# Attention on one core: the order of two PE steps of a unit, the values product and the spreading of 1/l

## What is computed

```
s = q @ k.T * SCALE + bias(head)           # causal, or dilated windows
p = exp(s - max(s)); l = sum(p)            # per query
out = (p @ v) / l
```

## Time and profile before

| what | value |
|---|---|
| median of 3 runs | 2630.19 us (2628.05 to 2633.6) |
| the profiled execution: its time, its span | 2626.38 us, 2624.3 us |
| mean granted TensorE clock | 0.992 of full speed |
| busy: PE, DVE, ACT, POOL | 97%, 43%, 21%, 42% |

### The profile page before, as it was taken

How to read it: one execution, slowest core, us unless ns; L and a number is a source line. 1 busy time by engine, 2 the same in 40 slices (tenths; PEclk the granted TensorE clock), 3 DMA queues, 4 the chain that set the end, 5 groups by cost and what they waited for, 6 DMA issues and landing times.

```text
span 2624.3 us, 42745 instructions
## 1 busy us (share of the span) xinstructions
PE 2556.8 (97%) x16331; PEld 2344.0 (89%) x16331; DVE 1133.9 (43%) x2258; ACT 550.1 (21%) x1266; POOL 1101.6 (42%) x702
## 2 busy tenths in 40 slices
PE   7999989999999999999999999899999999999999
PEld 5777756666899999999999987899999999999999
DVE  6636536667344333333333360553733333333333
ACT  5201136666322000000000051322300000000001
POOL 4234115566665444333344262435654443333440
PEclk9999999999999999999999999999999999999999
DMA  5223148767312111111111111111121111111111
GB/s 158 70 80 91 60 129 247 217 203 211 96 34 73 49 43 45 44 44 48 48 48 48 33 49 32 49 33 49 33 65 48 44 43 45 43 48 48 48 32 65
DMA packets 218459, 189.83 MB, mean 72 GB/s; under 512 B 29443, under 2 KB 171523, under 8 KB 217956
## 3 DMA queue, kind: packets, MB, share of 16 engines
q1 hardware_dynamic: 200996, 161.89, 21.2%
q10 hardware_dynamic: 17344, 26.35, 2.8%
HBM read 171.19 MB, written 17.01 MB: 72 GB/s over the span
## 4 chain that ended last, share of the span: by engine, by line
PE 69%; DVE 2%; POOL 2%; ACT 1%; issue 1%; ACTq 0%; POOLq 0%; PEldq 0%; DVEq 0%
PE ps L536 63%; PE ps L566 1%; PE ps L568 1%; PE ps L567 1%; ACT ps L2079 1%; POOL Xl L509 1%; POOL Wl L392 1%; POOL Wh L389 1%; DVE hs L479 0%; PE ps L2042 0%; POOL acc_sq L450 0%; PE ps L1265 0%; PE ps L1293 0%; PE ps L2211 0%; DVE VM_EARLY L2163 0%
## 5 line engine op out<-in xcount | busy, mean ns | idle before, releaser
L536 PE MATMUL ps<-Xh,Wh 128*128 128x256 f32 (+2 forms) x2712 | 872.6, 322 | 9.7 <-PE ps L536 3.3
L536 PE MATMUL ps<-Xl,Wh 128*128 128x256 f32 (+2 forms) x2712 | 867.4, 320 | 0.0
L536 PE MATMUL ps<-Xh,Wl 128*128 128x256 f32 (+2 forms) x2712 | 866.4, 319 | 0.0
L389 POOL TENSOR_TENSOR Wh<-raw,zeros 128x1024 fp32r<-128x1024 f32 x178 | 353.9, 1988 | 1072.5 <-PE ps L536 782.4
L536 PEld LDWEIGHTS ps<-Xh,Wh 128*128 128x128 f32 x2712 | 510.3, 188 | 15.6 <-issue 8.8
L536 PEld LDWEIGHTS ps<-Xh,Wl 128*128 128x128 f32 x2712 | 510.9, 188 | 0.0
L536 PEld LDWEIGHTS ps<-Xl,Wh 128*128 128x128 f32 x2712 | 510.3, 188 | 0.7
L392 POOL TENSOR_TENSOR Wl<-raw,Wh 128x1024 fp32r<-128x1024 f32 x178 | 440.9, 2477 | 14.0
L1839 DVE TENSOR_TENSOR Hl<-hf,Hh 128x392 fp32r<-128x392 f32 (+1 forms) x132 | 181.8, 1377 | 464.8 <-ACT Hh L1775 464.8
L536 PE MATMUL ps<-Hh,Wh 128*128 128x392 f32 (+2 forms) x1056 | 340.7, 323 | 1.2 <-DVE xT L1848 1.2
L536 PE MATMUL ps<-Hl,Wh 128*128 128x392 f32 (+2 forms) x1056 | 338.1, 320 | 0.0
(11 more groups left out here) (251 smaller groups left out, 2485.9 us busy)
## 6 DMA issues: line engine op xcount, KB each, us to landing
raw<-in_w_gate_up SPq DMA_DIRECT2D x88, 512.0 KB, 3.8
raw<-in_w_down SPq DMA_DIRECT2D x44, 512.0 KB, 3.5
kring<-in_cache_a_k SPq DMA_DIRECT2D x64, 256.0 KB, 3.6
ring<-in_cache_a_v SPq DMA_DIRECT2D x64, 256.0 KB, 3.1
raw<-in_w_in_even SPq DMA_DIRECT2D x20, 512.0 KB, 4.1
raw<-in_w_in_c SPq DMA_DIRECT2D x16, 512.0 KB, 3.9
xs<-in_x_prompt SPq DMA_DIRECT2D x8, 512.0 KB, 8.5
q_prompt<-zt ACTq DMA_DIRECT2D x16, 256.0 KB, 2.0
```

The source lines that it names most:

```text
L389: pool.tensor_tensor(h[:, :], r[:, :], zeros[:, :].to_broadcast([P, 1024]), ALU.add).then_inc(split_high, 1)
L536: ins = nc.tensor.matmul(out, w, x, start=(j == 0), stop=(j == len(pairs) - 1))
```

## The change

Within PE's iteration the order SP(u), W(u) becomes W(u), SP(u). In W three waits on `dch` are added, which counts DVE's sample steps: they hold W(u) until DVE has read what W(u - 1) left for the sample tokens in bank 6. Before, SP's wait for R stood for that. The other engines' programs are as they were.

```diff
@@ window(u)
                 positive_wait(pe, o_out, u)
+                for at, steps in ((TURN_AT, 4), (SPREAD_AT, 7), (SUM_AT + 1, 10)):
+                    if sample_at(u - 1, at) is not None:
+                        pe.wait_ge(dch, DCH * sample_at(u - 1, at) + steps)
                 if sample_at(u, VALUES_AT + 3) is not None:
@@ the loop of att_pe
-                spread_sums(u)
                 if u >= 0:
                     window(u)
+                spread_sums(u)
                 transpose_weights(u + 1, 0)
```

## The result

The changed kernel is slower: 2662.31 us (median of 4 runs, 2659.18 to 2663.83) against 2630.65 us for the kernel before (4 runs). The ratio is 1.0119, 95% interval 1.0103 to 1.0135. I had forecast 2661 and slower. The profiled execution took 2662.73 us with a span of 2660.2, so it is 35.9 us of span above the profiled one of before, 4 us more than the medians differ.

A forecast was written before the change was run, and what follows sets the result against it. PE was taken to bound the kernel. Lateness of 3.77 us per pair of heads, 30.2 over 8 pairs, became 31.2 with corrections; added to the profiled 2626.4 and 3.8 for the median, 2661 us, range 2638 to 2679.

The forecast's parts named there:

- PE bounds, and W was a cover: PE, busy 97% of the span, sets the end; W running on PE covers Rs and N1 on ACT.
- position 3: Units at this place in a pair of heads, without QK and S1: next T0 late by 1.1 us.
- The sum by position: Lateness of the next T0 over positions 0 to 7 in a pair of heads: 3.77 us, times 8 pairs 30.2.
- the term for T1: At position 3, T1 starts 1.33 us after T0 instead of 0.44: 0.89 us late.
- position 6: B0 of the next pair's widest unit hangs on SP, which moves behind a W of two blocks: 0.55 us late.
- (a): T0's second group needs the bank that Rs must first copy out: 0.25 us lost at positions 0, 1 and 2.
- (b): T1 may start when N1's sum is done, at 0.66 + N1 + 0.20 us after SP starts.
- (c): On ACT, C0 stands behind N1, starting 0.64 + N1 after SP; T1 of a two-group unit waits for C0.
- for the samples: W comes 0.25 us sooner while DVE's B0 comes later, at sample steps: +0.3 us each, +2.5 for 8.
- The clock: Rival: 16 pauses at positions 3 and 4 bring half clock, 27 us more, 2688 us; chance 0.06.
- The rival "faster": ACT and DVE keep up with later SP, PE's stalls on R go: 2622 us at most, 2625 likely; chance 0.07.
- The signs I had named: New T1 waits on S of 10 to 15 us, T0 waiting for Rs, attention about 31 us longer, later stages same to 1 us.

The follow-up runs named there:

- eighth kernel: Kernel before, with ACT's copy Rs(u) held until W(u) is done: 2645.94 us, 1.0062.
- tenth kernel: Changed kernel with N1 ahead of Rs everywhere, B0 free of SP, and SP writing a free quarter of bank 6 with its own semaphores: 2635.74 us, 1.0026.
- sixth: Changed kernel with B0 free of SP and N1 ahead of Rs, except in one of every eight units where Rs stays first: 2637.35 us, 1.0032.
- seventh kernel: Kernel before, with DVE's B0(u+2) held until W(u) is done: 2646.61 us, 1.0067.
- twelfth: Kernel before, with both B0(u+2) on DVE and Rs(u) on ACT held until W(u) is done: 2656.85 us, 1.0100.
- second: Changed kernel, with B0(u+2) waiting only for the transposes of unit u, no longer for SP(u): 2649.57 us, 1.0083.
- fifth: Kernel before, with B0(u+2) no longer waiting for SP(u): 2627.0 us, 0.9996.
- first kernel: Changed kernel, with ACT's copy Rs(u+1) moved behind the exponential N1(u+2): 2653.87 us, 1.0095.
- ninth kernel: Kernel before, with B0 free of SP and DVE's first sample reduction moved behind B1 and R: 2622.83 us, 0.9974.

## Why the prediction was right, and where it was not

**PE bounds, and W was a cover.** Right. T1 came 1.49 after SP at position 3 where I had 1.58, and holding only Rs in the kernel before gave T1's waits by itself (eighth kernel).

**The sum by position.** 30.2 forecast, 27.6 measured, with positions 2 to 4 carrying most in both. The two are not quite the same thing, since the 27.6 hold the waits of the samples and 1.7 us of half clock. The usual values, which are what the table speaks of, make 22.7 where it has 29.7 for the same distances: the terms were 7 us too high in all. Too high were position 3 (1.10 for 0.86), 5 (0.47 for 0.21) and 6 (0.55 for 0.15). At position 3 the term for T1 was 0.70 and not 0.89: T0 starts 0.35 behind SP and not 0.25, and T1 1.14 behind T0 instead of 0.44. The eighth kernel, which has this term alone, lost 0.73 there. At position 6 the term itself was about right: B0 starts 0.23 to 0.25 behind T0 where it started 0.18 to 0.53 ahead of it, 0.4 to 0.8 later in all seven units. But from B0 to the next T0 it takes less than before in six of the seven (at unit 54 5.03 and not 6.00). At unit 55 W, with a sample's step that it carries, had stood behind SP's wait for R, and now runs in it: T0(56) follows SP(55) by 0.52 instead of 1.50. I had put that win at nothing.

**A term that no run bears out is (a)**, 0.25 at positions 0, 1 and 2 for the bank of Rs. No wait of T0 for Rs is in the changed kernel's list, and SP's result in bank 6 (tenth kernel) left positions 0 and 1 as they were in the sixth. What their 0.16 each are was not tested. The bank counts at position 7 and only with N1 ahead of Rs.

**ACT's terms were too high and DVE's too low.** (a), (b) and (c) make 2.75 a pair, 22 us, and ACT's lateness alone costs 17 (eighth kernel). DVE's lateness, the terms at position 6 and for the samples, had 7 us together. How much it is depends on what stands beside it: 17 us alone (seventh kernel), 11 on top of ACT's (the twelfth less the eighth), and some 9 in the changed kernel, where freeing B0 won 11.3 (second) and the same edit wins 2.2 without the change (fifth). I had followed B0 to R only to see whether SP, itself later, would still find R ready, and had left out the sample's mask: QK's transposes wait for MV, which stands behind B0 and O on DVE. That wait went from 2.1 to 4.8 us, the longest from 0.9 to 1.9, and behind one of them came the half clock at 525.

**The clock.** I gave it 6 in 100 and said that no pause over 1 us but the old one was to be expected. Pauses of 1.95 (MV) and 1.98 (Lm) came:

```profile
524.32 0.66 PE L1229 MATMUL ps<-ident,qk 128*128 128x128 f32 x4 [1.95 <-DVE MV L1521]
```
```profile
499.18 0.28 PE L1300 MATMUL ps<-ident,Lm 128*16 128x128 f32 x1 [1.98 <-DVE Lm L1494]
```

Half clock at four places cost 8.3 us instead of 1.7; without the one at unit 0, which is not the change's, some 5 of the 35.9 us of the profiled span are what I had put to a rival. That the median still came out 1 us from the forecast is luck in part, errors that cancel: too much for the positions, too little for DVE and the clock, and 2 us that had arisen before the attention.

**The rival "faster".** Its premise was right, SP's waits for R halved. It failed where I had put it, in ACT's queue behind Rs, and on DVE as well.

**The signs I had named.** PE's waits on S at L1265 are new, but only 5.4 us in 11 places by PE's own row and not 10 to 15; those on ACT's copies rose from 2.2 to 5.0. T0's second group does not wait for Rs. SP's wait for R shrank outside position 7, to nothing. Rs starts under 0.55 behind SP in 63 of 64 units. The idle time in the attention is 31.8 us. The stages behind are not the same to 1 us, but 2.5 longer, by the clock.

## What to carry to other kernels

In a pipeline with fixed orders a long step covers whatever comes out of the short step ahead of it. Before a short step is put behind a long one, list every engine that waits for the short one (ACT, DVE and a PSUM bank here) and follow each to its last user, the small side jobs included, for each size of the long step. A stall in front of a step is often better won by shortening the queue that feeds it: moving one 0.67 us reduction out of DVE's chain, with B0 freed, won 0.26%, most of it at the two long stalls, while moving the waiting step lost 1.2%.

## What the runs showed of the hardware

I had taken one long pause to be needed for half clock. In the first kernel the clock fell behind two short ones, 0.70 before SP and 0.64 before T0's second group; the timeline of PE and the clock around it:

```profile
404.92 0.44 PE L1277 MATMUL ps<-ident,rl 128*64 128x128 f32 x4 [0.70 <-DVE rl L1464]
```
```profile
404.00:406.00 2.00, 1.21 (x12) 0.62 (x8) 1.93 (x9) 1.85 (x3) 0.70 (x2) 1.00 0.88 263
406.00:408.00 2.00, 1.36 (x7) 0.86 (x8) 1.43 (x6) 1.74 (x5) 1.07 (x1) 0.86 0.91 239
408.00:410.00 2.00, 2.00 (x8) 0.73 (x5) 0.62 (x1) 0.03 (x1) 1.92 (x4) 0.50 0.85 232
```

PE was busy 2.57 of the 4 us from 404 to 408, in the last of which the clock fell, and then worked at 0.50, that is at 1.2 GHz. In the changed kernel the 0.71 at the same place stood alone, and the clock stayed at 1.00. But two short pauses don't decide it either. The same pair stands in the same trace eight units on, 0.69 and 0.64, and the scores behind it take 1.13, full clock:

```profile
453.74 0.44 PE L1277 MATMUL ps<-ident,rl 128*64 128x128 f32 x4 [0.69 <-DVE rl L1464]
454.27 0.66 PE L1265 MATMUL ps<-ident,S 128*128 128x128 f32 x4
455.56 0.66 PE L1265 MATMUL ps<-ident,S 128*128 128x128 f32 x4 [0.64 <-ACT Rs L1394]
456.15 1.13 PE L1246 MATMUL ps<-KTr,QT 64*128 64x512 f32 x4
```

Nor does the length of one pause: in the changed kernel half clock came behind the 1.95 at 524.32 and not behind the 1.98 at 499.18:

```profile
499.00:504.00 5.00, 4.73 (x33) 2.80 (x35) 3.29 (x14) 3.80 (x8) 1.40 (x2) 1.00 0.89 278
```

So the same order of steps can meet the half clock at one unit and miss it at the next, and between 365 and 735 us the traces hold from 0 us of loss by it (ninth kernel) to 15 (twelfth). Each of these is one execution, so 1.7 us more or less of a stretch says nothing by itself. The Trainium skill, "TensorE: Matmul & The Clock Gate", in its section on the second failure mode, says that frequent short idles make the clock swing. This trace agrees at the first of the two places and not at the second. I had held it against the rule that the trace before showed none.
